# A two-part transformer kernel: the modulation rows' products taken out of the branch merges and put beside the output projection and the feed-forward

## The chip, the cores and the metric

The kernel runs on one NeuronCore of a Trainium2 chip, as one launch. The metric is the device time of the launch in microseconds (us); lower is better. The engines are TensorE (PE, matmuls into PSUM), VectorE (DVE), ScalarE (ACT), GpSimd (POOL) and SyncE (SP, which here issues all transfers between HBM and on-chip memory, in order, from one queue). Each engine works through its own program in order, and semaphores tie them together.

## The reference, cut

The first part is a transformer of two layers over 512 latent tokens (`LAT`) and 256 context tokens (`CTX`), each of width 1024. Every layer has six groups of modulation values, 1024 wide each, which are the product of a conditioning vector and a 1024 x 6144 matrix `w_ada`. The second part (two further layers, `second_block`) isn't touched by the change.

```python
for l in range(DEPTH):                    # DEPTH = 2
    last = l == DEPTH - 1
    mod_lat = (silu(c) @ w_ada[l] + b_ada[l])[:, None, :]
    mod_ctx = silu(c_ctx) @ w_ada[l] + b_ada[l]
    sh1, sc1, gt1, sh2, sc2, gt2 = jnp.split(mod_lat, 6, axis=-1)
    csh1, csc1, cgt1, csh2, csc2, cgt2 = jnp.split(mod_ctx, 6, axis=-1)
    h_lat = modulate(rms_norm(x_lat, g_mix[l]), sh1, sc1)
    ...
    # two attentions; mixer_outputs: merged = sigmoid(ga) * y_a + sigmoid(gb) * y_b; merged @ w_out
    if not last:
        x_ctx = x_ctx + cgt1 * o_ctx
    x_lat = x_lat + gt1 * o_lat
    h_lat = modulate(rms_norm(x_lat, g_ffn[l]), sh2, sc2)
    x_lat = x_lat + gt2 * conv_ffn(h_lat, p)
    if not last:
        ...                               # the same for x_ctx
```

All values are fp32. In the last layer the context stream ends after the attention, so from there on only the latent stream is worked on, and of its modulation groups 2 to 5 only the latent column is needed.

## The kernel before

**Tiling.** Activations lie transposed: 8 chunks of 128 features (`DC` = 8) by 768 tokens. A matmul of fp32 precision is made of three: both operands are split into a high part (ACT, a copy, L609 for weights) and a low part (DVE, a subtraction, L620), and PE multiplies high x high, high x low and low x high (L649, L650, L651). A weight block of up to 128 x 2048 words goes through these steps: SP loads it (L2980), ACT writes the high half (`act_prepare`), DVE the low half (`dve_prepare`), PE waits for the low half. There are two buffers for the raw and two for the split form (`N_SLOTS` = 2), so ACT can begin a block only when PE has ended the block before the last one, and the raw buffer is loaded anew when DVE has written the low half.

**Stages of a layer.** Attention; then the *merge* (`pe_merge`, `dve_merge` and so on): for each chunk m of 0 to 7 the branch products (block `w_br`, L1627 multiplies them by the gates), and for the even m also the gate products (block `w_in`; those of the odd m, `EARLY`, were made before and come back from HBM). POOL adds the two branches (L1643), and ACT and DVE split the sum (L1585, L1592). Then the *output projection* (`pe_out`, `dve_out`, L1709 adds into the residual `X`; the squares of `X` are summed for the next norm). Then the *feed-forward* in two halves of 11 hidden chunks: 22 steps (chunk x stream) of up-projection with a convolution (L1807, L1810), activation and product, followed by 8 chunks of down-projection (`dve_down`).

**Modulation rows.** A group of 1024 modulation values is 8 columns of 128 partitions; `w_ada` is kept in 24 blocks of 256 outputs per layer, and a *half* (layer, b, j) is 128 x 1024 words (512 KB) with the weights of one column. DVE makes a column with one multiply-and-sum over 1024 words per stream (L1504, two hardware rows: the operation and the read of its accumulator). In what follows such an operation is called a dot. Each dot waits for the one before it (they share a scrap output). Blocks 0 to 7 (groups 0 and 1) belong to the layer's start, 8 to 11 to the gate of the output projection (group 2), 12 to 19 to the feed-forward's shift and scale (groups 3 and 4), 20 to 23 to its gate (group 5). `ada_halves` says which halves are made where; `dve_ada` makes `count` of them and, after each, lets SP load the next into the same slot (`ada_load`, L3028: SP waits until the dots of the half in that slot are done). The merge has three slots, the feed-forward one (`row_all`).

**Order around the change.** DVE's program is written out by hand. In the merge, dots stand after the multiplications of the even chunks 0, 2 and 4 of each stream: with two streams 4 halves of 2 dots after every one of these six steps, in the second layer (one stream) 8 halves of 1 dot after each of the three. In the feed-forward of the first layer one half (2 dots) stands behind each of the steps 1 to 24, that is, all of the first half and the start of the second. `dve_mods_rest` adds the bias to groups 2 to 4 and makes the gain of the next norm.

## Time and profile before

| what | value |
|---|---|
| time, median of 3 runs | 3841.3 us (3839.09 to 3843.24) |
| the profiled execution | 3842.81 us, span in the profile 3841.1 us |
| mean granted clock of TensorE | 0.949 |
| PE busy | 3476.6 us (91%) |
| DVE busy | 1883.3 us (49%) |
| ACT busy | 1437.7 us (37%) |
| POOL busy | 310.1 us (8%) |
| dots (L1504) | 128 of about 1.27 us, 162.5 us |
| loads of `w_ada` by SP, 512 KB each | 80 |

PE's share is high, so what counts is where PE waits and at which clock it runs. The stages that matter here lie, in us of the span, at about 615 to 770 (merge of the first layer), 770 to 842 (its output projection), 842 to 1305 (its feed-forward, the second half from 1125 on) and 1899 to 2024 (merge of the second layer). A row of a timeline is start, duration, engine, line, operation, output<-input; the brackets at its end tell how long the engine had been idle before it and what released it.

### The profile page before, as it was taken

Reading aid. Unit: us, or ns where it says so; the run is one execution under the profiler, and the core shown is the slowest. Engines: PE = TensorE matmul, PEld = TensorE weight load, DVE = VectorE, ACT = ScalarE, POOL = GpSimd, SP = SyncE. Lnnn points to the kernel's source line nnn. Section 1 sums busy time; section 2 is a strip of 40 time slices with the busy share of each in tenths; the row PEclk is TensorE's granted clock in tenths of the full one; section 3 lists DMA queues with packets and bytes.
Section 4 is the critical chain, followed back from the end, with each engine's and each line's share of the span. In section 5 each row is a group of like instructions: output and inputs, shape, how many; then the busy total and the mean of one; then the engine's idle time right before and its main releaser. Section 6 shows DMA issues by size and latency. Waiting matters only on the chain.

```text
span 3841.1 us, 42569 instructions
## 1 busy us (share of the span) xinstructions
PE 3476.6 (91%) x17750; PEld 2903.1 (76%) x17750; DVE 1883.3 (49%) x2667; ACT 1437.7 (37%) x2201; POOL 310.1 (8%) x244
## 2 busy tenths in 40 slices
PE   7789898999999987888789999888999888879997
PEld 6678787788888876687667888766888677758886
DVE  5564655747735434546465645435333455333233
ACT  4453444234313334434524333434222345353222
POOL 0000000211101100000011101111000210230002
PEclk9899999999999998999989999999999889989999
DMA  5001114423322120011263322221222110112221
GB/s 199 33 20 49 44 58 159 152 96 121 120 74 70 57 78 32 18 58 59 86 218 121 126 100 89 97 78 69 94 99 93 69 45 33 45 44 95 97 92 67
DMA packets 74495, 321.96 MB, mean 84 GB/s; under 512 B 8896, under 2 KB 17856, under 8 KB 52288
## 3 DMA queue, kind: packets, MB, share of 16 engines
q1 hardware_dynamic: 74304, 319.25, 24.0%
q8 instruction: 140, 2.29, 0.3%
q14 instruction: 51, 0.42, 0.0%
HBM read 303.49 MB, written 15.73 MB: 83 GB/s over the span
## 4 chain that ended last, share of the span: by engine, by line
PE 71%; DVE 13%; ACT 8%; DMA 3%; issue 3%; POOL 2%; SPq 1%; POOLq 0%; ACTq 0%; DVEq 0%
PE psum L649 20%; PE psum L650 19%; PE psum L651 19%; DVE split_weights L620 2%; DMA arena<-w_ada_dram 2%; DVE arena L1504 2%; PE psum L1147 2%; ACT split_weights L609 1%; ACT arena L1280 1%; DVE arena L1436 1%; POOL arena L1943 1%; PE psum L1159 1%; DVE split_high L1450 1%; PE psum L662 1%; PE psum L663 1%
## 5 line engine op out<-in xcount | busy, mean ns | idle before, releaser
L649 PE MATMUL psum<-split_inputs,split_weights 128*128 128x512 f32 (+1 forms) x2872 | 1058.5, 369 | 17.6 <-DVE split_weights L620 14.0
L650 PE MATMUL psum<-split_inputs,split_weights 128*128 128x512 f32 (+1 forms) x2872 | 1048.2, 365 | 0.0
L651 PE MATMUL psum<-split_inputs,split_weights 128*128 128x512 f32 (+1 forms) x2872 | 1047.4, 365 | 0.0
L620 DVE TENSOR_TENSOR split_weights<-arena,split_weights 128x2048 fp32r<-128x2048 f32 (+3 forms) x246 | 505.0, 2054 | 406.5 <-ACT split_weights L609 406.2
L649 PEld LDWEIGHTS psum<-split_inputs,split_weights 128*128 128x128 f32 x2872 | 545.9, 190 | 113.8 <-DVE split_weights L620 16.3
L650 PEld LDWEIGHTS psum<-split_inputs,split_weights 128*128 128x128 f32 x2872 | 545.6, 190 | 86.9 <-issue 2.5
L651 PEld LDWEIGHTS psum<-split_inputs,split_weights 128*128 128x128 f32 x2872 | 545.1, 190 | 86.7
L609 ACT ACTIVATE split_weights<-arena 128x2048 fp32r<-128x2048 f32 (+3 forms) x246 | 413.6, 1683 | 177.1 <-PE psum L651 177.1
L649 PE MATMUL psum<-split_hidden,split_weights 128*128 128x512 f32 (+1 forms) x880 | 324.1, 368 | 0.9 <-DVE split_weights L620 0.9
L650 PE MATMUL psum<-split_hidden,split_weights 128*128 128x512 f32 (+1 forms) x880 | 323.9, 368 | 0.0
L651 PE MATMUL psum<-split_hidden,split_weights 128*128 128x512 f32 (+1 forms) x880 | 323.7, 368 | 0.0
L1280 ACT ACTIVATE arena<-psum,arena 128x768 f32<-128x768 f32 (+1 forms) x160 | 130.4, 816 | 249.6 <-DVE arena L1436 247.3
L1973 ACT ACTIVATE arena<-psum 128x512 f32<-128x512 f32 (+2 forms) x120 | 66.6, 556 | 372.4 <-PE psum L651 345.4
L649 PEld LDWEIGHTS psum<-split_hidden,split_weights 128*128 128x128 f32 x880 | 165.9, 189 | 29.5 <-DVE split_weights L620 2.0
L651 PEld LDWEIGHTS psum<-split_hidden,split_weights 128*128 128x128 f32 x880 | 165.9, 188 | 27.6
L650 PEld LDWEIGHTS psum<-split_hidden,split_weights 128*128 128x128 f32 x880 | 165.9, 189 | 27.5
L671 ACT ACTIVATE arena<-arena 128x512 f32<-128x512 f32 (+1 forms) x135 | 79.1, 586 | 283.0 <-DVE arena L1832 102.2
L1504 DVE CUSTOM_DVE_ANT_0 arena<-arena 128x1024 f32<-128x1024 f32 x128 | 162.5, 1269 | 26.4 <-DMA arena<-w_ada_dram 19.9
L1147 PE MATMUL psum<-split_high 128*128 128x512 f32 (+3 forms) x864 | 143.2, 356 | 31.2 <-ACT arena L1280 24.8
L1643 POOL TENSOR_TENSOR arena<-arena 128x512 f32<-128x512 f32 (+1 forms) x24 | 45.7, 1913 | 1358.1 <-DVE arena L1627 1358.1
L1147 PEld LDWEIGHTS psum<-split_high 128*128 128x128 f32 (+1 forms) x864 | 114.0, 200 | 52.7 <-issue 15.1
L1775 ACT ACTIVATE arena<-psum,arena 128x512 f32<-128x512 f32 (+1 forms) x132 | 90.9, 699 | 160.1 <-PE psum L651 158.1
(327 smaller groups left out, 5094.4 us busy)
## 6 DMA issues: line engine op xcount, KB each, us to landing
arena<-w_up_dram SPq DMA_DIRECT2D x44, 1024.0 KB, 4.8
arena<-ffn_up_dram SPq DMA_DIRECT2D x44, 1024.0 KB, 4.8
arena<-w_ada_dram SPq DMA_DIRECT2D x80, 512.0 KB, 3.9
arena<-w_in_dram SPq DMA_DIRECT2D x32, 1024.0 KB, 5.0
arena<-w_down_dram SPq DMA_DIRECT2D x32, 704.0 KB, 4.1
arena<-ffn_down_dram SPq DMA_DIRECT2D x32, 704.0 KB, 4.1
arena<-od_w_in_dram SPq DMA_DIRECT2D x13, 1024.0 KB, 4.8
arena<-w_ada_dram SPq DMA_DIRECT2D x8, 1024.0 KB, 12.5
```

The source lines that it names most:

```text
L609: act.e.activation(ws[:, i % N_SLOTS, 0, 0:nk * w], raw_view(key), ACT.Copy).then_inc(*w_hi(*key))
L620: dve.e.tensor_tensor(ws[:, i, 1, 0:nk * w], raw_view(key), ws[:, i, 0, 0:nk * w].bitcast(F32), ALU.subtract).then_inc(*w_lo(*key))
L649: pe.e.matmul(dst, a[0], b[0], start=i == 0, stop=False)
L650: pe.e.matmul(dst, a[0], b[1], start=False, stop=False)
L651: ins = pe.e.matmul(dst, a[1], b[0], start=False, stop=i == n - 1)
L671: act.e.activation(row, view, ACT.Square).then_inc(*squared(site, s, c))
L1147: ins.append(pe.e.matmul(dst, a[rows_at, :], b[rows_at, :], start=i == 0, stop=i == 2))
L1280: act.e.activation(row[:, 0:p["keys"]], psum[:, b:b + p["keys"]], ACT.Exp, bias=st[:, sub:sub + 1], accum_out=st[:, 2 + sub:3 + sub]).then ...
L1504: dve.e.tensor_tensor_reduce(rstd_all, ADA[slots[n % len(slots)]], wide[:, s, :], 1.0, 0.0, ALU.mult, ALU.add, mods[al][:, 2 * b + j, s:s ...
L1643: pool.e.tensor_tensor(MG[:, m, s[0]:s[1]], PG[:, 2 * (i % 2), 0:n], PG[:, 2 * (i % 2) + 1, 0:n], ALU.add).then_inc(*added("merge", l, m, s))
L1775: act.e.activation(y, banks.at("up", l, half, m, s, g)[:, 0:n], ACT.Identity, bias=vc(l, "conv_b", ch), scale=vc(l, "conv_w", 2 * FC + ch) ...
L1973: act.e.activation(dst, banks.at(*key)[:, cols], func, **more).then_inc(*banks.back(key, copied, *key))
```

## The change

- The second layer's 24 halves of blocks 8 to 19 (one dot each) leave its merge. They now follow, in the first layer's feed-forward, behind the halves that stood there. There are then 48 halves instead of 24: the first 21 stand as before behind steps 1 to 21, the other 27 are spread over the 22 steps of the second half, one behind most steps and two behind five of them (the LAT steps of chunks 0, 2 and 4 and the CTX steps of chunks 6 and 8). The slot is still one.
- Of the first layer's 24 halves of the merge, the last 8 (blocks 16 to 19, group 4, two dots each) go to its output projection, one half behind each chunk's CTX step, with two slots that the merge had used and a scrap area of their own. The merge keeps 16 halves: 3, 2, 3, 2, 3, 3 behind its six steps in place of 4 each.
- The bias and the gain of group 4 move in the first layer from the merge to the end of the output projection.
- Work, loads and bytes are the same in number: 128 dots, 80 loads.

```diff
@@ ada_halves
-    streams = 1 if layer == DEPTH - 1 else 2
-    if stage == "merge":
-        return [(layer, b, j, streams) for b in range(8, 20) for j in range(2)]
-    out = [(layer, b, j, streams) for b in range(20, 24) for j in range(2)]
-    if layer < DEPTH - 1:
-        out += [(layer + 1, b, j, 2) for b in range(8) for j in range(2)]
-    return out
+    def halves(of_layer, start, end, streams):
+        return [(of_layer, b, j, streams) for b in range(start, end) for j in range(2)]
+
+    if layer == DEPTH - 1:
+        return halves(layer, 20, 24, 1) if stage == "ffn" else []
+    return {"merge": halves(layer, 8, 16, 2), "out": halves(layer, 16, 20, 2),
+            "ffn": halves(layer, 20, 24, 2) + halves(layer + 1, 0, 8, 2) + halves(layer + 1, 8, 20, 1)}[stage]
@@ ada_load
                 errand("ada", slots[n % len(slots)], part["halves"][n][0:3], part["halves"][n - len(slots)]
-                       if n >= len(slots) else None)
+                       if n >= len(slots) else part["in_slot"][n] if "in_slot" in part else None)
@@ dve_ada
-                    dve.e.tensor_tensor_reduce(rstd_all, ADA[slots[n % len(slots)]], wide[:, s, :], 1.0, 0.0, ALU.mult,
+                    dve.e.tensor_tensor_reduce(part.get("junk", rstd_all), ADA[slots[n % len(slots)]], wide[:, s, :], 1.0, 0.0, ALU.mult,
@@ dve_merge
-                    dve_mods_rest(l)
+                    dve_mods_rest(l, [2, 3] if part["halves"] else [2, 3, 4])
@@ dve_out
             errand("load_x", l)
+            part = dict(halves=ada_halves(l, "out"), loads=[], done=[])
+            if part["halves"]:
+                in_slot = dict((n % 3, half) for n, half in enumerate(ada_halves(l, "merge")))
+                part.update(in_slot=[in_slot[i] for i in ADA_OUT], junk=spent)
+                for _ in ADA_OUT:
+                    ada_load(ADA_OUT, part)
...
+                if s == mine(l)[-1]:
+                    dve_ada(ADA_OUT, part, 1)
+            if part["halves"]:
+                dve_mods_rest(l, [4])
@@ dve_ffn
-                if i:
-                    dve_ada(ADA_FFN, part, 1)
+                half_n = len(up_steps(l)) // 2
+                due = i if i < half_n else half_n - 1 - (half_n - 1 - len(part["halves"])) * (i - half_n + 1) // half_n
+                dve_ada(ADA_FFN, part, due - len(part["done"]))
```

**DVE, merge of the second layer.** `ISA arena<-arena 128x1024` is a dot and `ISA arena 128x1` the read of its accumulator. Before, the last two of the eight dots behind chunk 0 are followed by the multiplications of chunk 1, two weight blocks, chunk 2, another block and the next eight dots:

```order
L1504 ISA arena<-arena 128x1024
L1504 ISA arena 128x1
L1504 ISA arena<-arena 128x1024
L1504 ISA arena 128x1
L1627 TENSOR_TENSOR arena<-arena,psum 128x512 x2
L620 TENSOR_TENSOR split_weights<-arena,split_weights 128x1024 x2
L1627 TENSOR_TENSOR arena<-arena,psum 128x512 x2
L620 TENSOR_TENSOR split_weights<-arena,split_weights 128x2048
L1504 ISA arena<-arena 128x1024
```

Now, from chunk 0 on (the lines have moved: L1630 is L1627 of before, L622 is L620):

```order
L1630 TENSOR_TENSOR arena<-arena,psum 128x512 x2
L622 TENSOR_TENSOR split_weights<-arena,split_weights 128x2048
L1630 TENSOR_TENSOR arena<-arena,psum 128x512 x2
L622 TENSOR_TENSOR split_weights<-arena,split_weights 128x1024 x2
L1630 TENSOR_TENSOR arena<-arena,psum 128x512 x2
L622 TENSOR_TENSOR split_weights<-arena,split_weights 128x2048
```

No dot stands between a chunk's multiplications and the next weight block.

**SP, second half of the first layer's feed-forward.** Before, two `w_ada` loads stand among the loads of this half, and the rest are weight blocks:

```order
L2980 DMA arena<-w_down_dram 128x1408 x5
L2980 DMA arena<-w_up_dram 128x2048 x4
L3028 DMA arena<-w_ada_dram 128x1024 x2
L2980 DMA arena<-w_up_dram 128x2048 x7
L2980 DMA arena<-w_down_dram 128x1408 x8
```

Now (L2996 is L2980 of before, L3044 is L3028):

```order
L2996 DMA arena<-w_down_dram 128x1408 x5
L2996 DMA arena<-w_up_dram 128x2048 x4
L3044 DMA arena<-w_ada_dram 128x1024 x3
L2996 DMA arena<-w_up_dram 128x2048
L3044 DMA arena<-w_ada_dram 128x1024 x2
L2996 DMA arena<-w_up_dram 128x2048
L3044 DMA arena<-w_ada_dram 128x1024 x3
L2996 DMA arena<-w_up_dram 128x2048
L3044 DMA arena<-w_ada_dram 128x1024 x2
L2996 DMA arena<-w_up_dram 128x2048
```

Two or three loads of halves stand between each two weight blocks, and each waits for the dots of the half before it.

**DVE, the same place.** Behind the LAT step of chunk 2 of this half (L1830 ends a step; L1815 before) there are now two halves, where before there was none:

```order
L1825 SCALAR_TENSOR_TENSOR arena<-psum,arena 128x511
L1830 TENSOR_TENSOR split_hidden<-arena,split_hidden 128x512
L1506 ISA arena<-arena 128x1024
L1506 ISA arena 128x1
L1506 ISA arena<-arena 128x1024
L1506 ISA arena 128x1
L1822 SCALAR_TENSOR_TENSOR arena<-psum,arena 128x255
```

The CTX step's convolution (L1822) now stands behind both dots, and behind the load between them.

## Rows read from the trace of the kernel before

**Rows 1.** The page's chain that ended last: share of the span by line.
```profile
PE psum L649 20%; PE psum L650 19%; PE psum L651 19%; DVE split_weights L620 2%; DMA arena<-w_ada_dram 2%; DVE arena L1504 2%; PE psum L1147 2%; ACT split_weights L609 1%; ACT arena L1280 1%; DVE arena L1436 1%; POOL arena L1943 1%; PE psum L1159 1%; DVE split_high L1450 1%; PE psum L662 1%; PE psum L663 1%
```

**Rows 2.** Windows: us; busy PE, PEld, DVE, ACT, POOL; granted clock, DMA share, GB/s.
```profile
770.00:840.00 70.00, 69.30 (x392) 60.19 (x391) 22.57 (x27) 20.40 (x29) 14.62 (x14) 1.00 0.33 117
845.00:1030.00 185.00, 184.55 (x1041) 162.36 (x1040) 143.82 (x219) 74.98 (x109) 20.22 (x20) 0.99 0.32 108
1110.00:1290.00 180.00, 180.00 (x1045) 159.73 (x1044) 89.87 (x121) 62.80 (x87) 19.54 (x19) 1.00 0.20 67
```

**Rows 3.** PE timeline; last row: waits of 1922 to 2024, total, times, longest.
```profile
654.43 0.79 PE L649 MATMUL psum<-split_inputs,split_weights 128*128 128x512 f32 x1 [5.78 <-DVE split_weights L620]
...
694.58 0.80 PE L649 MATMUL psum<-split_inputs,split_weights 128*128 128x512 f32 x1 [4.09 <-DVE split_weights L620]
...
734.77 0.79 PE L649 MATMUL psum<-split_inputs,split_weights 128*128 128x512 f32 x1 [3.74 <-DVE split_weights L620]
...
PE psum L649 <- DVE split_weights L620: 17.4, 3, 7.1
```

**Rows 4.** Windows behind five of the six restarts, columns as in rows 2.
```profile
654.43:660.00 5.57, 5.57 (x15) 4.38 (x16) 5.33 (x8) 1.60 (x3) 0.54 (x1) 0.57 0.54 154
694.58:700.50 5.92, 5.92 (x14) 4.65 (x15) 5.56 (x9) 1.67 (x3) 0.54 (x1) 0.52 0.62 206
734.77:740.00 5.23, 5.23 (x17) 4.24 (x18) 5.01 (x7) 1.47 (x3) 0.54 (x1) 0.71 0.53 148
1943.79:1949.40 5.61, 5.61 (x13) 4.45 (x14) 2.19 (x2) 0.00 (x0) 1.09 (x1) 0.50 0.70 242
1975.81:1980.50 4.69, 4.69 (x12) 3.69 (x13) 2.18 (x1) 0.00 (x0) 1.09 (x1) 0.53 0.50 181
```

**Rows 5.** Timelines of DVE, ACT, DVE in the second layer's merge: start, duration.
```profile
1942.52 3.44 DVE L620 TENSOR_TENSOR split_weights<-arena,split_weights 128x1024 fp32r<-128x1024 f32 x2
...
1952.27 1.92 ACT L609 ACTIVATE split_weights<-arena 128x2048 fp32r<-128x2048 f32 x1 [11.29 <-PE psum L651]
...
1954.22 2.35 DVE L620 TENSOR_TENSOR split_weights<-arena,split_weights 128x2048 fp32r<-128x2048 f32 x1 [1.19 <-ACT split_weights L609]
```

**Rows 6.** DVE timeline in the first layer's merge.
```profile
679.90 1.22 DVE L1504 CUSTOM_DVE_ANT_0 arena<-arena 128x1024 f32<-128x1024 f32 x1
...
689.16 1.23 DVE L1504 CUSTOM_DVE_ANT_0 arena<-arena 128x1024 f32<-128x1024 f32 x1
...
691.58 0.75 DVE L1627 TENSOR_TENSOR arena<-arena,psum 128x256 f32<-128x256 f32 x2
692.25 2.28 DVE L620 TENSOR_TENSOR split_weights<-arena,split_weights 128x2048 fp32r<-128x2048 f32 x1
```

**Rows 7.** PE timeline: the first matmul behind a shorter wait.
```profile
1510.31 0.50 PE L649 MATMUL psum<-split_high,split_weights 128*128 128x512 f32 x1 [2.25 <-DVE split_high L1383]
```

**Rows 8.** DVE timeline in the first layer's feed-forward, first half.
```profile
943.29 2.29 DVE L620 TENSOR_TENSOR split_weights<-arena,split_weights 128x2048 fp32r<-128x2048 f32 x1
...
953.61 0.48 DVE L1807 SCALAR_TENSOR_TENSOR arena<-psum,arena 128x255 f32<-128x255 f32 x1
...
957.45 1.23 DVE L1504 CUSTOM_DVE_ANT_0 arena<-arena 128x1024 f32<-128x1024 f32 x1
...
959.87 2.29 DVE L620 TENSOR_TENSOR split_weights<-arena,split_weights 128x2048 fp32r<-128x2048 f32 x1
```

**Rows 9.** w_ada loads, issue to landing: windows 840:1050, 1100:1290 and 1900:2020.
```profile
DMA to landing us min/median/max: 3.4/3.7/4.0
...
DMA to landing us min/median/max: 3.9/4.3/4.6
...
DMA to landing us min/median/max: 3.5/5.1/6.1
```

**Rows 10.** DVE timeline at the end of the first layer's output projection.
```profile
836.76 0.48 DVE L1709 SCALAR_TENSOR_TENSOR arena<-psum,arena 128x256 f32<-128x256 f32 x1 [2.12 <-PE psum L651]
842.04 1.42 DVE L857 SCALAR_TENSOR_TENSOR arena<-arena 128x512 f32<-128x512 f32 x2 [4.79 <-ACT arena L712]
```

More of the change, by code:

```diff
@@ L1512, in build @@
         OH = merge_lay(2, 8, N_TOK, words=split_words)
+        spent = Layout(arena, merge_lay.at, merge_lay.at + D)(D)
         PG = merge_lay(4, N_TOK)
@@ L1518, in build @@
         ADA = [row_all, after_o(D), after_o(D)]
-        ADA_MERGE, ADA_FFN = (0, 1, 2), (0,)
+        ADA_MERGE, ADA_OUT, ADA_FFN = (0, 1, 2), (1, 2), (0,)
         def merge_steps(l):
@@ L1691, in act_out @@
                 i = mine(l).index(s)
-                act.wait_ge(dotted, *last_dot(l, "merge"))
+                if ada_halves(l, "merge"):
+                    act.wait_ge(dotted, *last_dot(l, "merge"))
                 act.wait_ge(conv, "out", l, m, s)
@@ L1715, in pool_out, with dve_mods_rest @@
                 pool_square_summed(("x1", l), s, m, DC, s[1] - s[0], mine(l).index(s))
-        def dve_mods_rest(l):
+        def dve_mods_rest(l, groups):
             streams = len(mine(l))
-            dve.wait_ge(dotted, *last_dot(l, "merge"))
-            dve_mods(l, [2, 3, 4], streams)
-            dve_gain(l, 1, 4, "g_ffn", streams)
+            dve.wait_ge(dotted, l, 4 * groups[-1] + 3, 1, streams - 1)
+            dve_mods(l, groups, streams)
+            if groups[-1] == 4:
+                dve_gain(l, 1, 4, "g_ffn", streams)
         ffn_lay = Layout(arena, ffn_rows_at, arena_n)
```

## The prediction

> **What bounds the kernel now.** I began with the page's shares and the chain that ended last. PE's three split matmuls are 58% of that chain; behind them, at 2% each, stand the dots (L1504), the loads of `w_ada` and the low halves of weights (L620) [rows 1]. So PE bounds the whole, and the dots are on the path somewhere: 128 dots are 162.5 us of DVE, of which 2% of the span (some 77 us) lie on the chain. Next I looked at windows by stage, to see where PE is not busy. In the output projection and in both halves of the first layer's feed-forward it is: 69.30 of 70 us, 184.55 of 185, 180.00 of 180, at a granted clock of 0.99 to 1.00 [rows 2]. The first half of that feed-forward carries 42 of the dots (21 halves) and still loses nothing, with DVE busy 143.8 of 185 us; the second half has DVE busy 89.9 of 180. The waits of PE tell where time is lost: in the merges PE waits six times for a low half of weights (L620), 5.78, 4.09 and 3.74 us in the first layer, and three times, 17.4 us together, in the second [rows 3]. L620 is late there because DVE's program has eight dots in front of it. After each wait PE runs for about 5 us at a granted clock of 0.50 to 0.71, the lower of its two levels (1.2 of 2.4 GHz) for most of it [rows 4]. Time is thus lost twice, in the wait and behind it.
>
> **Second layer's merge, all 24 dots gone.** The waits are 17.4 us [rows 3]. The slow stretches cost (1 - clock) x length: 5.61 x 0.50 = 2.8 and 4.69 x 0.47 = 2.2 [rows 4]; the third I take as their mean, 2.5. Sum 24.9 us. What is late next is the preparation of a gate block of 2048 words: ACT may start when PE has ended a branch block (1952.2), DVE has finished at 1954.22 + 2.35 = 1956.6, so 4.4 us later [rows 5], while PE works on the next branch block of 24 matmuls at some 0.23 us, 5.4 us. One microsecond of slack, three times over; so I count no new wait there. The block before it is no danger: the two L620 that today follow the dots [rows 5] are ready for DVE long before PE's 11 us of gate products end. The SP queue loses 24 loads that each wait for a dot; the gates' and weights' loads behind them can only come earlier. Bounds: 22 (a microsecond of new wait per gate block) to 26.
>
> **First layer's merge, 16 of 48 dots gone.** Between the end of a branch product and the next gate block, DVE has eight dots, two multiplications and L620. With six dots the third piece starts at the 689.16 of today's seventh dot instead of 691.58: 2.42 us earlier [rows 6]. This comes three times, once for each of PE's waits: they fall from 5.78, 4.09, 3.74 to 3.4, 1.7 and 1.3, a gain of 7.3 us. The slow stretches: behind a wait of 2.25 us the first matmul took 0.50 us [rows 7], where the six restarts above begin with 0.79 or 0.80 [rows 3]. So I expect no slow stretch behind the waits of 1.7 and 1.3 us, which gives back 5.92 x 0.48 = 2.8 and 5.23 x 0.29 = 1.5 [rows 4]. The first, 5.57 x 0.43 = 2.4, becomes at 3.4 us of wait about what it is behind 3.74 today, 1.5: 0.9 less. Sum 7.3 + 4.3 + 0.9 = 12.5 us. Bounds: 7.3 if the clock gives nothing, 14.0 if all three stretches go.
>
> **Output projection of the first layer: nothing.** Eight halves of 2.42 us go where PE is busy 69.30 of 70 us and DVE 22.57 [rows 2]; DVE has over 40 us free and adds 19.4. The two loads that are put ahead of a `w_out` block pass it by 1 MB, but that block isn't needed for two further pairs of chunks. The delicate place is the end: the next norm's first operation starts at 842.04, released by ACT, 4.8 us after the last residual addition (836.76 + 0.48) [rows 10]. The last half's two dots end 2.42 later at 839.7; the four 128x8 operations for group 4 have 2.4 us and would fit even at half a dot's length each. Bounds: 0 to 2 us lost.
>
> **Second half of the first layer's feed-forward, 24 dots more.** Here something is paid. DVE's cycle for a chunk (two steps) in the first half, from L620 to L620, is 959.87 - 943.29 = 16.58 us with two halves of 2.42 us (957.45 to 959.87) [rows 8]. That is also PE's time for a chunk, so 4.8 us of dots a chunk are just what DVE's chain bears. Without dots the chain takes 11.7 us. A half of one dot takes 1.2, so chunks with two single halves need 14.1 us. But a step with two halves has one slot for both: behind the first dot comes a load, and only then the second dot. A load takes 3.7 us from issue to landing in the first half of this feed-forward (21 of them), 4.3 in the second (two of them: 3.9 and 4.6), 5.1 in the second layer's merge [rows 9]. At 3.8 us such a chunk takes 14.1 + 1.2 + 3.9 = 19.2 us, and with its light neighbour 33.3, against 33.2 of PE: level, 0.1 us lost, five times. The first chunk is worse, since its three halves still have two dots each: 16.6 + 2.4 + 3.9 = 22.9 us, 6.3 over PE's, less the 4.9 us of slack (16.6 - 11.7) that the chain has when it enters: 1.4 us. Together 2 us at 3.8 us a load. At 4.3 us each double step takes 0.5 more, and so does each chunk's second half, which starts its wait one CTX part (957.45 - 953.61 = 3.8 us) after the first: 1.5 us a pair, some 7 to 9 in all. I take 3.5, near the lower end, since the 21 loads at 3.7 ran among the same weight loads as these will. Bounds 0 and 15 (4.6 us a load).
>
> **The sum.** 24.9 + 12.5 - 0 - 3.5 = 33.9 us. The profiled execution took 3842.8 us (span 3841.1), so 3808.9; the median of the runs, 3841.3, is 1.5 lower, and that is what is to be compared: 3807.4 us.
>
> **Rivals.** (a) *The loads in the second half take the gain of a stage back.* At 4.6 us a load, each pair of chunks needs 0.8 + 1.6 = 2.4 us more, five times, plus the opening: about 14.5 us in place of 3.5. The result is 3818. For it speaks that both of today's samples there are above 3.7, and that the slot is single. Against it that the DMA engines are a fifth busy there, a third in the first half [rows 2]. The Trainium skill, "DMA: Bandwidth & Descriptors", section "Rules for kernel authors", asks that a load be issued early, work be done, and its semaphore be waited for late; the double steps do the contrary. By that rule the whole load of each double step would be paid, 5 x 3.8 = 19 us, and the time would be 3823; the trace of today agrees with the rule in the second layer's merge, where the dots wait, and the slack of DVE's chain is what it leaves out here.
>
> (b) *Slower.* The same place, but with loads as long as the longest in the second layer's merge, 6.1 us [rows 9]. Then the double chunks take 19.2 + 2.3 + 2.3 and the light ones 14.1 + 2.3, 40.2 against 33.2: 7 us a pair, 38 in all, and each of the five waits of PE is long enough to be followed by a slow stretch of 2.4 us as in rows 4, 12 us. With the opening 54 us, against 37.4 gained: 3858 us. It decides from about 5.7 us a load upward. Against it: that length occurs where three slots are loaded at a time, at a DMA load well above this one.
>
> (c) *The clock doesn't follow.* PE still falls to the lower level behind the short waits of the first layer: 4.3 + 0.9 us less, 3812.6 us. For it: in rows 4 the third wait, 3.74 us, is hardly shorter than the second and its stretch is shorter by half, so there is no sharp rule to be read.
>
> (d) *It doesn't do what it says.* If PE's waits in the second layer's merge were set by the gates' loads or by ACT and only shown as L620, they would remain. The rows speak against it: ACT's high half was written before and DVE took both blocks back to back for 3.44 us [rows 5]. If all 17.4 + 7.5 us remained: 3832, and within 0.2% of before only if the first layer's gain went too.
>
> **How the numbers follow.** The forecast with (c) inside it, 3799 to 3815: 0.70. (a), 3815 to 3826: 0.19. (d) and other partial failures, 3826 to 3834: 0.03. No change: 0.04. (b): 0.04. A measurement of this kernel can tell about 0.2% (7.7 us) from no change. Faster by more than that is 0.92, within it 0.04, slower 0.04. The range 3799 to 3825 holds about 8.5 in 10: below, the bounds 26 + 14 - 0 = 40 us; above, 22 + 7.3 - 2 - 11 = 16 us.
>
> **What would show it.** In the profile after: no dot between 1900 and 2024 less what was gained, and no wait of PE for L620 over 1 us there; the merge of the second layer shorter by 25 us at a clock near 1.00. In the first layer three waits of some 3.4, 1.7 and 1.3 us, and a clock near 1.00 behind the last two. In the output projection eight times two dots, PE without waits, the step at today's 842.04 still released by ACT. In the second half of the feed-forward DVE busy some 30 us more, five waits of dots for a load of about 3.8 us, and waits of PE for L620 of 0 to 1.5 us each. The prediction is wrong if those last waits sum to over 10 us, if the clock falls behind them, or if the second layer's merge keeps a wait of several microseconds with another releaser.

## The result

The changed kernel takes 3809.36 us (median of 4 runs, 3805.58 to 3812.43) against 3840.2 us before (4 runs, 3838.57 to 3843.24): a ratio of 0.9917, 95% interval 0.9903 to 0.9932. The forecast was 3807.4 us. A second set of 4 runs gave 3807.68 us and 0.9912 (0.9895 to 0.9928). The profiled execution took 3812.43 us, with a span of 3810.7; before it was 3842.81 and 3841.1.

Two rows of the page of the changed kernel, the share of PE and the chain by line, answer to [rows 1]. The line numbers have moved by 2 to 16: L651 to L653 are the three split matmuls, L622 the low half of a weight, L1506 the dot, L3044 its load, L1630 the branch multiplication.

```profile
PE 3468.2 (91%) x17750; PEld 2896.8 (76%) x17750; DVE 1881.7 (49%) x2667; ACT 1436.6 (38%) x2201; POOL 317.9 (8%) x244
...
PE psum L651 20%; PE psum L652 20%; PE psum L653 20%; DVE split_weights L622 2%; DVE arena L1506 2%; PE psum L1149 2%; DMA arena<-w_ada_dram 1%; DVE arena L1438 1%; ACT arena L1282 1%; POOL arena L1959 1%; ACT split_weights L611 1%; DVE split_high L1452 1%; PE psum L1161 1%; PE psum L664 1%; PE psum L665 1%
```

PE is busy 8.4 us less than before (3468.2 for 3476.6) though it does the same matmuls, so some of them ran at a higher clock. The rest of the 30.4 us of span is waiting that has gone. The loads of `w_ada` are down from 2% to 1% of the chain.

The PE timeline shows its restarts after waits for a low half of a weight. Three are in the first layer's merge and one in the second half of its feed-forward; they answer to [rows 3].

```profile
652.24 0.51 PE L651 MATMUL psum<-split_inputs,split_weights 128*128 128x512 f32 x1 [3.12 <-DVE split_weights L622]
...
688.77 0.50 PE L651 MATMUL psum<-split_inputs,split_weights 128*128 128x512 f32 x1 [1.09 <-DVE split_weights L622]
...
723.68 0.50 PE L651 MATMUL psum<-split_inputs,split_weights 128*128 128x512 f32 x1 [1.09 <-DVE split_weights L622]
...
1146.36 0.50 PE L651 MATMUL psum<-split_inputs,split_weights 128*128 128x512 f32 x1 [0.99 <-DVE split_weights L622]
```

The waits in the first merge were 5.78, 4.09 and 3.74 us and are now 3.12, 1.09 and 1.09. In the second layer's merge, none of the three of together 17.4 us is left. The one at its opening, 2.91 us before, 2.87 now, stays; it stands ahead of the first of the old three and no dot is in front of it. The windows behind the three restarts, and one long window in the second layer's merge (columns as in [rows 2], to be read against [rows 4]):

```profile
652.24:657.00 4.76, 4.76 (x14) 3.77 (x15) 4.55 (x7) 0.59 (x2) 0.54 (x1) 0.64 0.40 128
688.77:694.00 5.23, 5.23 (x23) 4.34 (x24) 4.66 (x7) 1.51 (x3) 0.55 (x1) 1.00 0.58 191
723.68:729.00 5.32, 5.32 (x23) 4.43 (x24) 5.11 (x7) 1.46 (x3) 0.55 (x1) 1.00 0.52 153
1919.00:1990.00 71.00, 71.00 (x310) 57.91 (x309) 30.68 (x34) 22.24 (x28) 10.93 (x7) 1.00 0.36 128
```

Behind the two short waits the clock is 1.00, where it was 0.52 and 0.71. Behind the 3.12 us it still falls (0.64). In the second layer's merge PE is busy for 71.00 of 71 us at full clock.

The windows of the stages that took the dots (output projection, then the two halves of the first layer's feed-forward), against [rows 2]:

```profile
758.00:828.00 70.00, 68.83 (x390) 59.80 (x388) 45.39 (x62) 20.16 (x29) 19.58 (x14) 1.00 0.50 174
832.00:1017.00 185.00, 184.31 (x1036) 162.04 (x1037) 144.14 (x219) 74.75 (x109) 20.25 (x20) 0.99 0.32 108
1097.50:1277.50 180.00, 179.01 (x1033) 158.47 (x1033) 107.16 (x156) 60.95 (x85) 18.26 (x18) 1.00 0.35 121
```

DVE is busy 45.39 us for 22.57 in the output projection, and 107.16 for 89.9 in the second half of the feed-forward (the window ends before the last of the moved dots), and PE hardly notices: 68.83 of 70 and 179.01 of 180 us.

### Where the time went, stage by stage

A stage is measured from one restart of PE to another, which every profile shows: from the last wait for the attention's split outputs (634.86 us in the kernel before) to the first matmul of the feed-forward (844.48), from there to the second layer's first matmul (1407.58), to its last gate products before the merge (1897.19), and to its own feed-forward (2072.00). All numbers are us of the profiled executions.

| kernel | first merge and output projection | first feed-forward | second attention | second merge and output projection |
|---|---|---|---|---|
| before | 209.6 | 563.1 | 489.6 | 174.8 |
| changed | 196.7 | 564.1 | 494.6 | 149.6 |
| changed, again (e10) | 196.7 | 564.6 | 490.8 | 147.7 |
| e1, second layer's halves only | 209.7 | 563.5 | 489.2 | 147.7 |
| e2, first layer's halves only | 197.4 | 562.5 | 486.1 | 174.8 |
| e3, before with 3 and 5 | 206.6 | 562.5 | 485.7 | 175.2 |
| e4, changed with 2 and 3 | 189.8 | 563.5 | 488.2 | 149.6 |
| e5, changed with 4 and 1 | 209.0 | 563.9 | 495.6 | 149.8 |
| e6, changed, packed feed-forward | 196.7 | 607.9 | 492.0 | 149.9 |
| e7, changed, no double step | 197.3 | 562.4 | 489.6 | 149.6 |
| e8, 2 and 3, no double step | 189.8 | 562.5 | 493.6 | 147.8 |
| e9, before, dots spread inside the merges | 189.9 | 563.2 | 492.2 | 160.0 |

The merges gained 12.9 and 25.2 us and the feed-forward lost 1.0. The second attention, in which nothing was changed, took 5.0 us more in the first profile; the experiments come back to that (e10).

The last stage has two values where no dot is left in it, 149.6 to 149.9 us and 147.7 to 147.8. They differ by the clock behind the wait that opens the merge, which is not a wait for dots. The windows behind it in the changed kernel (wait of 2.87 us) and in e10, the same program (2.90 us):

```profile
1914.37:1919.00 4.63, 4.63 (x13) 3.64 (x14) 3.46 (x4) 1.53 (x3) 3.19 (x1) 0.64 0.43 123
```

```profile
1910.31:1915.00 4.69, 4.69 (x20) 3.86 (x21) 3.94 (x4) 1.52 (x3) 3.20 (x1) 1.00 0.37 128
```

At 0.64 the 4.63 us cost 1.7 us more than at full clock.

### The profile page after: what moved, and what is told of

The parts are those of the page before. It is cut to its first block, busy times and chain, and to the rows that moved or that the text cites. A ratio compares the mean times of both kernels' runs of the same rounds, so it can differ in the third digit from the quotient of the medians.

```text
span 3810.7 us, 42568 instructions
## 1 busy us (share of the span) xinstructions
PE 3468.2 (91%) x17750; PEld 2896.8 (76%) x17750; DVE 1881.7 (49%) x2667; ACT 1436.6 (38%) x2201; POOL 317.9 (8%) x244
## 4 chain that ended last, share of the span: by engine, by line
PE 71%; DVE 14%; ACT 8%; issue 2%; DMA 2%; POOL 2%; SPq 1%; POOLq 0%; ACTq 0%; DVEq 0%
PE psum L651 20%; PE psum L652 20%; PE psum L653 20%; DVE split_weights L622 2%; DVE arena L1506 2%; PE psum L1149 2%; DMA arena<-w_ada_dram 1%; DVE arena L1438 1%; ACT arena L1282 1%; POOL arena L1959 1%; ACT split_weights L611 1%; DVE split_high L1452 1%; PE psum L1161 1%; PE psum L664 1%; PE psum L665 1%
## 5 line engine op out<-in xcount | busy, mean ns | idle before, releaser
L651 PE MATMUL psum<-split_inputs,split_weights 128*128 128x512 f32 (+1 forms) x2872 | 1057.4, 368 | 11.6 <-DVE split_weights L622 7.9
L653 PE MATMUL psum<-split_inputs,split_weights 128*128 128x512 f32 (+1 forms) x2872 | 1046.2, 364 | 0.0
L622 DVE TENSOR_TENSOR split_weights<-arena,split_weights 128x2048 fp32r<-128x2048 f32 (+3 forms) x246 | 505.6, 2056 | 423.4 <-ACT split_weights L611 423.0
L651 PEld LDWEIGHTS psum<-split_inputs,split_weights 128*128 128x128 f32 x2872 | 545.3, 190 | 107.6 <-DVE split_weights L622 9.9
L653 PEld LDWEIGHTS psum<-split_inputs,split_weights 128*128 128x128 f32 x2872 | 544.4, 190 | 85.9
L651 PE MATMUL psum<-split_hidden,split_weights 128*128 128x512 f32 (+1 forms) x880 | 324.1, 368 | 0.6 <-DVE split_weights L622 0.5
L653 PE MATMUL psum<-split_hidden,split_weights 128*128 128x512 f32 (+1 forms) x880 | 323.7, 368 | 0.0
L651 PEld LDWEIGHTS psum<-split_hidden,split_weights 128*128 128x128 f32 x880 | 165.9, 189 | 29.3 <-DVE split_weights L622 1.6
L653 PEld LDWEIGHTS psum<-split_hidden,split_weights 128*128 128x128 f32 x880 | 165.9, 188 | 27.6
L1506 DVE CUSTOM_DVE_ANT_0 arena<-arena 128x1024 f32<-128x1024 f32 x128 | 165.2, 1290 | 28.6 <-DMA arena<-w_ada_dram 24.0
L696 POOL TENSOR_TENSOR arena<-arena 128x512 f32<-128x512 f32 (+1 forms) x60 | 76.4, 1275 | 953.3 <-ACT arena L673 953.3
L1646 POOL TENSOR_TENSOR arena<-arena 128x512 f32<-128x512 f32 (+1 forms) x24 | 45.0, 1883 | 1326.0 <-DVE arena L1630 1326.0
```

The lines of the kernel that those rows point to most:

```text
L622: dve.e.tensor_tensor(ws[:, i, 1, 0:nk * w], raw_view(key), ws[:, i, 0, 0:nk * w].bitcast(F32), ALU.subtract).then_inc(*w_lo(*key))
L651: pe.e.matmul(dst, a[0], b[0], start=i == 0, stop=False)
L653: ins = pe.e.matmul(dst, a[1], b[0], start=False, stop=i == n - 1)
L696: pool.e.tensor_tensor(acc, acc, rows.at(site, s, c)[:, 0:w], ALU.add).then_inc(*rows.back((site, s, c), pooled, site, s, c))
L1506: dve.e.tensor_tensor_reduce(part.get("junk", rstd_all), ADA[slots[n % len(slots)]], wide[:, s, :], 1.0, 0.0, ALU.mult, ALU.add, mods[al][ ...
L1646: pool.e.tensor_tensor(MG[:, m, s[0]:s[1]], PG[:, 2 * (i % 2), 0:n], PG[:, 2 * (i % 2) + 1, 0:n], ALU.add).then_inc(*added("merge", l, m, s))
```

## The experiments

The theory to be tested is A: PE's waits in a merge are set by the dots that stand in DVE's program ahead of the next weight block's low half, and by the slow clock behind the waits. Rival C: it is the amount of DVE work in the merge. Rival B: the moved halves bring a cost of some 5 us into the second layer's attention. Rival D: the load between two halves of a step is hidden.

### e1: only the second layer's halves moved

```diff
-    return {"merge": halves(layer, 8, 16, 2), "out": halves(layer, 16, 20, 2),
+    return {"merge": halves(layer, 8, 20, 2), "out": [],
```

One more line puts the bias and the gain of group 4 back into the merge.

> Only the second layer's 24 halves are moved, behind the steps of the first layer's feed-forward as in the change; the first layer's merge keeps all 24 halves. Theory A (the waits of PE in a merge are the dots that stand ahead of the next weight block, and the clock stretch behind them): the second layer's merge gains about 25 us, the second half of the feed-forward loses the 1.0 us of PE wait that the profile of the change showed there: 3840.2 - 24 = 3816 us. The three waits of the first layer's merge are back at 5.8, 4.1 and 3.7 us. Theory B (a fixed cost of some 5 us in the second layer's attention comes with these moved halves): the attention of the second layer, 489.6 us from the first up-norm matmul to the merge before, is 494 to 495 us again, and the gain is only 19 us: 3821 us.

Measured: 3818.67 us (4 runs), ratio 0.9937 (0.9919 to 0.9956). The second merge took 147.7 us, the first 209.7 with waits of 5.70, 4.09 and 3.73 us, and the feed-forward has one wait of 1.04 us. The second attention took 489.2 us: these halves had moved, and in this execution the 5 us were not there. But the profiled execution, 3813.7 us, was the fastest of the four (up to 3830.69), and the median lies between the two expectations. So the profile speaks against B and the times don't; e10 comes back to it.

### e2: only the first layer's halves moved

```diff
-        return halves(layer, 20, 24, 1) if stage == "ffn" else []
+        return {"merge": halves(layer, 8, 20, 1), "out": [], "ffn": halves(layer, 20, 24, 1)}[stage]
...
-            "ffn": halves(layer, 20, 24, 2) + halves(layer + 1, 0, 8, 2) + halves(layer + 1, 8, 20, 1)}[stage]
+            "ffn": halves(layer, 20, 24, 2) + halves(layer + 1, 0, 8, 2)}[stage]
```

Two more lines give the feed-forward one half a step as before and put the second layer's bias and gain of group 4 back.

> Only the first layer's 8 halves are moved to its output projection; the second layer's merge keeps its 24 halves and the feed-forward its 24. Theory A: 12.5 to 13 us less than before, 3827 to 3828 us, with PE's waits in the first layer's merge at 3.1, 1.1 and 1.1 us, and in the second layer's merge 17.4 us as before. Theory B (the loss in the second layer's attention comes with the halves of the second layer): that attention is 489.6 us as before. If it comes with neither part but differs from run to run, it is somewhere between 489 and 495 us here and in the run before this.

Measured: 3826.07 us (6 runs), ratio 0.9958 (0.9945 to 0.9971), 16 us for 12.5 to 13 expected. The first merge took 197.4 us (12.2 less). PE's restarts there follow waits of 4.06, 1.09 and 1.09 us. The first is longer than the changed kernel's 3.12, yet the restart comes at the same place, 16.9 us after the stage's start in both: PE was quicker ahead of the wait. The second merge is as before, by its row of waits (total, times, longest), 16.3 us for 17.4:

```profile
PE psum L651 <- DVE split_weights L622: 16.3, 3, 6.5
```

The parts add up by stage. The profiled execution took 17.9 us less than that of before: 12.2 of them are the first merge, 0.6 the feed-forward and 3.5 the second attention (486.1 us).

### e3: the kernel before, 3 and 5 halves in place of 4 and 4

```diff
-            shares = [3 * (s == LAT) + 2 * (s == CTX) if m not in EARLY and m < LAST_GATE else 0 for m, s in steps]
+            shares = [3 * (s == LAT) + 5 * (s == CTX) if m not in EARLY and m < LAST_GATE else 0 for m, s in steps]
```

> The kernel before, with nothing moved out of the first layer's merge; only the split between the two streams is changed: 3 halves behind the LAT step and 5 behind the CTX step of the chunks 0, 2 and 4, instead of 4 and 4. Theory A (what counts is only how many dots stand between a LAT branch product and the gate block's L620, not how many the merge holds): PE waits 3.1, 1.1 and 1.1 us there, and the kernel is 12 us faster than before although all 48 dots are still there: 3828 us. Rival C (the merge's DVE work as a whole is the bound, and moving 16 dots out is what gained): no gain, 3840 us, with new waits of PE for L620 at the branch blocks behind the CTX steps.

Measured: 3838.46 us (10 runs), ratio 0.9990 (0.9980 to 0.9999). The expected 12 us came to 3.0 in the stage. Neither A nor C as written is right. The rows of waits in the first layer's merge:

```profile
PE psum L649 <- DVE arena L1627: 7.3, 3, 3.0
PE psum L649 <- DVE split_weights L620: 5.7, 3, 3.2
```

The waits for L620 fell from 13.6 to 5.7 us, as A says (3.17, 1.45 and 1.09). But PE now waits elsewhere, three times, for the multiplications L1627. One of the three restarts, and DVE's timeline ahead of it (the first of ten dots in a row, the last one, and the multiplications of chunk 3):

```profile
707.22 0.39 PE L649 MATMUL psum<-split_inputs,split_weights 128*128 128x256 f32 x1 [2.92 <-DVE arena L1627]
```

```profile
692.95 1.76 DVE L1504 CUSTOM_DVE_ANT_0 arena<-arena 128x1024 f32<-128x1024 f32 x1
...
705.34 1.23 DVE L1504 CUSTOM_DVE_ANT_0 arena<-arena 128x1024 f32<-128x1024 f32 x1
...
706.49 1.94 DVE L1627 TENSOR_TENSOR arena<-arena,psum 128x512 f32<-128x512 f32 x4
```

PE restarts 0.7 us after L1627 began. The ten dots stand behind a CTX step, and behind them come the four multiplications that read the odd chunk's branch products out of PSUM. The program gives PE's products there six banks in turn, and PE waits until the next one is free. So a row of dots behind a CTX step has a deadline of its own. Ten dots miss it. Eight don't: the kernel before has rows of eight behind its CTX steps and e4 one, and neither has a wait for these multiplications. That the wait is one of a 256-column product is what the row shows; that the bank is what they wait for is read from the releaser and the program's wait, and e9 tests it.

### e4 and e5: the changed kernel with the halves of the merge at other places

```diff
-            shares = [3 * (s == LAT) + 2 * (s == CTX) if m not in EARLY and m < LAST_GATE else 0 for m, s in steps]
+            shares = [2 * (s == LAT) + 3 * (s == CTX) if m not in EARLY and m < LAST_GATE else 0 for m, s in steps]
```

e5 has 4 and 1 in the same line.

> The changed kernel with 2 halves behind the LAT step and 3 (at the end 4) behind the CTX step of chunks 0, 2 and 4, instead of 3 and 2; the same 16 halves in the first layer's merge. Theory A: each of the three waits of PE loses another 2.4 us: 3.1, 1.1, 1.1 become 0.7, 0 and 0, and the clock stretch behind the first (4.76 us at 0.64) goes: 5.3 - 0.7 + 1.7 = 6.3 us less than the changed kernel, 3803 us. Rival C (amount, not place): no difference to the changed kernel, 3809 us.

> The changed kernel with 4 halves behind the LAT step and 1 (at the end 2) behind the CTX step of chunks 0, 2 and 4; the same 16 halves in the first layer's merge. Theory A (place): the waits are those of before, 5.8, 4.1 and 3.7 us, with a clock of 0.5 to 0.7 behind them, and the first layer's part of the gain is gone although 16 dots have left the merge: 12.5 us more than the changed kernel, 3822 us. Rival C (amount): 3809 us, as the changed kernel.

Measured: e4 3799.83 us, 0.9883 (0.9869 to 0.9898); e5 3818.04 us, 0.9938 (0.9923 to 0.9953). The amount is that of the changed kernel in both, 32 dots. The times expected by A were 3803 and 3822 us. By stage, e4 has 189.8 us, 6.9 less than the changed kernel (6.3 expected), and e5 has 209.0, which is the kernel before (209.6), although 16 dots have left the merge. The waits of PE for L622 there, first e4, then e5:

```profile
PE psum L651 <- DVE split_weights L622: 0.5, 1, 0.5
```

```profile
PE psum L651 <- DVE split_weights L622: 13.3, 3, 5.8
```

Rival C falls for this merge: taking a third of the dots out was worth 0.6 us when eight were left behind each LAT step, so the change's gain there comes with the step from 8 to 6 dots at those places. With e3 that is only half of the rule: the dots that leave a LAT step must not make a row of ten behind a CTX step. The window behind e4's only restart shows no slow clock behind 0.48 us:

```profile
650.43:655.40 4.97, 4.97 (x22) 4.08 (x23) 4.76 (x7) 0.00 (x0) 0.55 (x1) 1.00 0.58 181
```

### e6: every step of the second half with two halves

```diff
-                due = i if i < half_n else half_n - 1 - (half_n - 1 - len(part["halves"])) * (i - half_n + 1) // half_n
+                due = i if i < half_n else half_n - 1 + 2 * (i - half_n + 1)
```

> The changed kernel with two halves behind every step of the second half of the first layer's feed-forward until the 27 are done (13.5 steps), so that every step has a load between its two halves. Theory A (with one slot a second half in a step costs DVE the whole load, about 3.8 us, and then one dot): DVE's chain takes 11.7 + 2 x 6.3 = 24.3 us a chunk against 16.6 of PE, 27.9 for the first chunk; over 6.75 chunks 168.6 against 116.2 us, less the 4.9 us of slack: 45 to 48 us more than the changed kernel, 3855 us, slower than before. A slow clock behind the waits costs nothing more, since PE then waits for DVE in any case. Rival D (PE's six banks and the two weight buffers take it up): under 10 us more.

Measured: 3852.27 us (8 runs), ratio 1.0022 (1.0011 to 1.0032), slower than before. The feed-forward took 607.9 us, 43.8 more than the changed kernel (45 to 48 expected). PE's waits in that half, its first three restarts, and the window behind the first of them:

```profile
PE psum L651 <- DVE split_weights L622: 32.7, 7, 6.1
```

```profile
1149.71 0.80 PE L651 MATMUL psum<-split_inputs,split_weights 128*128 128x512 f32 x1 [5.93 <-DVE split_weights L622]
...
1173.64 0.80 PE L651 MATMUL psum<-split_inputs,split_weights 128*128 128x512 f32 x1 [5.11 <-DVE split_weights L622]
...
1197.18 0.80 PE L651 MATMUL psum<-split_inputs,split_weights 128*128 128x512 f32 x1 [4.74 <-DVE split_weights L622]
```

```profile
1149.71:1154.50 4.79, 4.79 (x13) 3.82 (x14) 2.76 (x4) 1.14 (x2) 1.27 (x1) 0.58 0.77 267
```

From restart to restart it is 23.9 and 23.5 us, where the chain of DVE was reckoned at 24.3. So the chain's reckoning holds: with one slot, a second half in a step costs the whole load. The slow clock adds nothing to that, as was expected: the six stretches of 4.8 us at 0.55 to 0.68 cost 12 us, the waits are 32.7 us, and together they are about the 44 us by which DVE's chain is longer. By that reckoning PE would at full clock only have waited longer. Rival D falls.

### e7: no step with two halves

```diff
+                if half == 0 and m < 6:
+                    dve_ada(ADA_FFN, part, 1)
...
-                due = i if i < half_n else half_n - 1 - (half_n - 1 - len(part["halves"])) * (i - half_n + 1) // half_n
+                due = i if i < half_n else i + 6
```

The first two lines stand at the end of a chunk in `dve_down`, which is given `part` for it.

> The changed kernel without any step that has two halves: six of them go behind the first six chunks of the down-projection of the first half, the others one behind each step. Theory A: the one wait of PE in the second half of the feed-forward (0.99 us, at the third chunk) goes, and with it the waits of dots for loads there (20.6 us of DVE); the time falls by 1 us, 3808 us, within what a measurement tells.

Measured: 3807.36 us, ratio 0.9905 (0.9891 to 0.9920). The feed-forward took 562.4 us, 1.7 less than with the double steps, and PE has no wait for L622 in its second half. The difference of the times is within what a measurement tells; the stage shows it. Over all profiles the stage is 563.5 to 564.6 us in the five with five double steps, where PE waits once for 0.71 to 1.71 us, and 562.4 to 563.2 in the six with none.

### e8: both

The edits of e4 and e7 together.

> Both: 2 and 3 halves behind the LAT and CTX steps of the first layer's merge, and no step with two halves in the feed-forward. Theory A: the two gains add, 6.3 + 1.0 us less than the changed kernel: 3802 us, about 1.0% faster than before. Rival C: 3808 us.

Measured: 3797.62 us, ratio 0.9879 (0.9863 to 0.9896), the fastest of all. It is not to be told from e4 (0.9883). Both ratios lie below the changed kernel's interval.

### e9: nothing moved out, the dots spread inside the merges

```diff
-            shares = [3 * (s == LAT) + 2 * (s == CTX) if m not in EARLY and m < LAST_GATE else 0 for m, s in steps]
+            share_of = {(0, LAT): 2, (0, CTX): 3, (1, LAT): 0, (1, CTX): 3} if l == 0 else {(0, LAT): 3, (1, LAT): 5}
+            shares = [share_of[m % 2, s] if m < LAST_GATE else 0 for m, s in steps]
```

> The kernel before with nothing moved out of either merge; only the places inside the merges are changed. First layer: 2 halves behind the LAT step and 3 behind the CTX step of chunks 0, 2 and 4, and 3 behind the CTX step of chunks 1, 3 and 5. Second layer: 3 halves behind each even and 5 behind each odd chunk up to 5. All 72 dots stay in the merges. Theory A2 (what counts is the length of every unbroken row of dots against the deadline behind it: the gate block's L620 behind a LAT step, and the multiplications of the odd chunk that free PE's banks behind a CTX step): no wait of PE over 1 us in the first layer's merge (stage 190 us from the last restart of the branch products to the feed-forward, 209.6 before) and none but the first in the second layer's (149.6 us, 174.8 before): 3842.4 - 19.8 - 25 = 3797 us, as fast as the best so far, without moving a dot to another stage. Rival C (the merges can't hold 48 and 24 dots: DVE or the loads' wait in three slots is the bound): waits remain in the second layer's merge, where five dots behind an odd chunk need loads of about 5 us each, and the time is 3810 us or more.

Measured: 3803.07 us (4 runs), ratio 0.9901 (0.9884 to 0.9918), between the two expectations. The two layers answer differently. The profiled execution was the slowest of the four, 3811.34 us, so this too is read by stage. The waits of PE for L620, first in the first layer's merge, then in the second's:

```profile
PE psum L649 <- DVE split_weights L620: 0.4, 1, 0.4
```

```profile
PE psum L649 <- DVE split_weights L620: 7.8, 4, 5.4
```

In the first layer all 48 dots stay and 0.4 us of waiting is left; the stage takes 189.9 us, 19.7 less than before and as little as e4. The longest row has six dots, and the waits for L1627 of e3 are gone with the rows of ten. In the second layer the stage takes 160.0 us, 14.8 less than before but 10.4 more than with the dots moved out. DVE's timeline there, and the loads' time to landing, show why:

```profile
1942.28 1.23 DVE L1504 CUSTOM_DVE_ANT_0 arena<-arena 128x1024 f32<-128x1024 f32 x1
...
1951.55 1.23 DVE L1504 CUSTOM_DVE_ANT_0 arena<-arena 128x1024 f32<-128x1024 f32 x1 [8.04 <-DMA arena<-w_ada_dram]
...
1954.08 1.22 DVE L620 TENSOR_TENSOR split_weights<-arena,split_weights 128x1024 fp32r<-128x1024 f32 x1
```

```profile
DMA to landing us min/median/max: 3.7/5.9/10.6
```

A dot waited 8.04 us for its load, and the low half of the next block stood behind it; the loads took 5.9 us in the median and up to 10.6. So the second layer's merge is held by its loads, as rival C has it there, and the first layer's is not. No run has the first layer's dots spread as here and the second layer's moved out.

### e10: the changed kernel again, for the second attention

No edit.

> The changed kernel once more, for its second layer's attention, which took 494.6 us in its first profile and 489.6 us before. If that is a cost of the change, it is again 494 to 495 us; if it differs from run to run (theory A), it lies anywhere in the 485.7 to 495.6 us that the profiles of kernels with and without the moved halves have shown. The merges are as in the first profile: 196.7 and 149.6 us.

Measured: 3807.68 us, ratio 0.9912 (0.9895 to 0.9928). The stage took 490.8 us. Windows of the second attention from its first matmul to its last gate products, in the kernel before, the changed one, the changed one again, and e3:

```profile
1407.58:1897.19 489.61, 410.57 (x2331) 345.17 (x2331) 265.70 (x421) 219.72 (x386) 0.00 (x0) 0.91 0.13 43
```

```profile
1396.13:1890.69 494.56, 412.94 (x2330) 346.15 (x2331) 265.77 (x421) 219.76 (x386) 0.00 (x0) 0.91 0.13 43
```

```profile
1396.17:1886.98 490.81, 410.97 (x2331) 345.39 (x2331) 265.65 (x421) 219.74 (x386) 0.00 (x0) 0.91 0.13 43
```

```profile
1406.74:1892.47 485.73, 405.01 (x2330) 340.68 (x2331) 265.58 (x421) 219.78 (x386) 0.00 (x0) 0.92 0.13 43
```

DVE and ACT are busy for the same time within 0.2 us in all four. PE's busy time moves between 405.01 and 412.94 us, and the stage by somewhat more. Over all profiles the stage is 485.7 to 495.6 us, with both layers' halves moved (488.2 to 495.6), with either alone (486.1, 489.2) and with none (485.7, 489.6, 492.2). The same program gave 494.6 and 490.8, so a fixed 494 to 495 us is not what the change costs. That the difference lies in how the clock's two levels fall on the many short waits there is an inference from PE's busy time; no run here sets the clock.

But a smaller or less regular cost isn't excluded, and the times speak for one. Take from each kernel's median time its three changed stages of the table. With the second layer's halves moved, 2895.3 to 2899.0 us are left (eight sets of runs); without, 2890.0 (e9), 2891.4 (e2), 2894.2 (e3) and 2892.7 to 2895.0 (before, by its medians of 3840.2 to 3842.5). The means are some 5 us apart and the two groups don't overlap. By profiles, of which there is one per set, the second attention alone is 3.3 us longer in the mean with these halves moved (491.7 to 488.4), with the ranges overlapping. So B stays open: where such a cost would arise, no run shows.

## Why the prediction was right, point by point

- **Second layer's merge, 24.9 us.** Measured 25.2 (and 27.1 in e1 and e10). All three waits are gone. The stage's two values differ by the clock behind its opening wait, which the forecast left out. The reckoned slack of a microsecond for each gate block held: no new wait came in their place [rows 5].
- **First layer's merge, 12.5 us.** Measured 12.9. The waits forecast at 3.4, 1.7 and 1.3 us came out at 3.12, 1.09 and 1.09, and the clock behind the last two stayed at 1.00, which rival (c) doubted. The stretch behind the first was 4.76 us at 0.64: 1.7 us, for 1.5 forecast. So the waits gave 8.3 us for 7.3 and the clock 5.0 for 5.2; the output projection's half microsecond comes off. The step argued the right way, by the dots between a LAT product and the gate block, as e4 and e5 show. What it didn't see is that no dot had to leave the merge for it (e9).
- **Output projection, nothing.** PE lost half a microsecond by its window (68.83 of 70 us for 69.30). DVE's timeline at its end, against [rows 10]:

```profile
824.28 0.48 DVE L1719 SCALAR_TENSOR_TENSOR arena<-psum,arena 128x256 f32<-128x256 f32 x1 [2.12 <-PE psum L653]
...
825.94 1.23 DVE L1506 CUSTOM_DVE_ANT_0 arena<-arena 128x1024 f32<-128x1024 f32 x1
...
829.56 1.41 DVE L859 SCALAR_TENSOR_TENSOR arena<-arena 128x512 f32<-128x512 f32 x2 [1.90 <-ACT arena L714]
```

  The last residual addition, the last dot, and the next norm's first operation, which waited 1.90 us for ACT. The last half fits with 1.9 us to spare; the four small operations take half a microsecond, well under the bound of 2.4.
- **Second half of the feed-forward, 3.5 us lost.** The direction was right and the size too high: 1.0 us in the first profile and 1.5 in the second, 1.7 and 2.2 against e7, which has no double step. PE waited once, at the third chunk, for 0.99 us (1.4 us late by the forecast). DVE's timeline of the first chunk (last dot of its first half, first of its second, then the next block's low half) and the loads of that half:

```profile
1129.36 1.23 DVE L1506 CUSTOM_DVE_ANT_0 arena<-arena 128x1024 f32<-128x1024 f32 x1
...
1135.57 1.23 DVE L1506 CUSTOM_DVE_ANT_0 arena<-arena 128x1024 f32<-128x1024 f32 x1 [4.98 <-DMA arena<-w_ada_dram]
...
1144.02 2.29 DVE L622 TENSOR_TENSOR split_weights<-arena,split_weights 128x2048 fp32r<-128x2048 f32 x1
```

```profile
DMA to landing us min/median/max: 3.4/3.7/4.9
```

  The dot waited 4.98 us here; the loads took 3.7 us in the median, as in the first half, and 4.9 at most. The other four double steps waited 3.54 to 4.00 us for theirs. The term was sized between 3.8 and 4.3 us a load; the trace shows the lower value, at which the working itself had 0.1 us for a pair. Rival (a)'s 4.6 us throughout didn't come, and no run has it.
- **The sum.** By stages of the profiled executions it is -12.9 - 25.2 + 1.0 = -37.1 us for -33.9 forecast. The span fell by 30.4 only, since the second attention took 5.0 us more and what lies outside the four stages 1.8. The forecast had neither. So the time, 2 us off, is in part luck: 3 us of gain that were not forecast met a loss of 7 us that was not forecast either. How much of that loss is difference between executions and how much a cost of the moved halves is open (e10). The range has two slips of its own: its upper end takes 11 us for the feed-forward where the bound was 15, which would give 3829, and the lower end by its own bounds is 3801, not 3799.
- **Rivals.** (b)'s mechanism, DVE's chain grown longer than PE's work, is real (e6 is slower than before by it), but it took 13 double steps, each with a wait of 3.5 to 5.0 us for its load, where the changed kernel has five. (d) didn't happen.
- **The rule on early loads.** The five double steps waited 20 us of DVE for their loads and cost the stage 1.0 to 1.5 us, not 5 x 3.8 = 19, since DVE's chain had slack; in e6 the slack was used up. "DMA: Bandwidth & Descriptors" of the Trainium skill, "Rules for kernel authors", has a DMA issued early and waited for late; e6 agrees with it, as each double step paid its load.

## What to carry to other kernels

Side work on an engine that others wait for should be counted by the unbroken row between what releases it and the next instruction that is waited for, not by its share of the stage: here rows of 8 dots behind the LAT steps cost the first layer's merge 20 us, rows of 4 there and of up to 8 behind a CTX step nothing (e4, e9), and a third of the work could leave with hardly a gain (e5). Try to spread it inside its stage before moving it out; move it when its loads, and not its own time, are what the others would wait for (e9, second layer). With one buffer, the second of two pieces of such work behind each other pays for the whole load: five such places fitted into the slack of DVE's chain, thirteen cost 44 us (e6).

## What the runs showed of the hardware that wasn't expected

- The granted clock behind a wait is not told by the wait's length alone. In the merges and the second half of the feed-forward the first matmul took 0.50 to 0.51 us behind waits of up to 1.71 us, and also behind 3.04 to 3.12 us (e6, e10, the changed kernel), but then the next 4.7 us ran at 0.64. It took 0.72 behind 3.17 us (e3) and 0.79 to 0.80 behind 3.73 us and more.
- The wait that opens the second layer's merge was 2.84 to 2.92 us in every profile. The first matmul behind it took 0.50 to 0.51 us in eleven of the twelve and 0.80 in e2. The 4.6 to 4.7 us behind it ran at 0.60 to 0.66 in nine profiles and at 1.00 in three (e1, e8, e10). The changed kernel and e10 are the same program, with 0.64 in the one profile and 1.00 in the other.
- At the end of the first attention, where PE waits several times within a few microseconds, the first matmul took 0.79 us behind 1.74 us (e5) and 0.80 behind 1.47 (e3). Each of these restarts came 2.4 to 2.7 us after another, whose wait was 1.63 and 1.90 us. The changed kernel has 1.47 us in the same place, 2.4 us after a restart behind 1.01 us, and there it took 0.51.
- The same program's second attention took 490.8 and 494.6 us in two executions, with DVE and ACT busy for the same time. Over all profiles it is 485.7 to 495.6 us, which is more than this change's smaller terms. Changed stages have to be compared by themselves; but a stage is known from one execution here, and what the rest of the kernel does is told only by the medians (e10).
